# Unscaled attention probabilities, turned by a product with the identity times the inverse sums

## What is computed

```
# block 1, differential attention: 4 heads, two score parts each
s = where(visible, q @ k.T * scale - slope * dist, -inf)
p = softmax(s)
p = p[:, 0] - lam * p[:, 1]
o = p @ v
# block 1, cross attention to 256 memory tokens: 4 heads of 256
p = softmax(q @ k.T * 256 ** -0.5); o = p @ v
# block 2: 8 heads of 64, keys chosen by a top-k index
p = softmax(where(valid, q @ k_sel.T * scale, -inf)); o = p @ v_sel
# block 3, forgetting attention: 8 heads of 64
p = softmax(where(causal, q @ k.T * scale + c_i - c_k, -inf)); o = p @ v
```

## Time and profile before

| | |
|---|---|
| three runs | 2840.22, 2843.74, 2840.40 us, median 2840.40 us |
| the profiled execution | 2841.07 us, span 2839.8 us, mean granted TensorE clock 0.981 |
| PE busy | 2715.2 us, 96% |
| PEld busy | 2328.0 us, 82% |
| DVE / ACT / POOL busy | 1598.5 us (56%) / 1055.0 us (37%) / 639.4 us (23%) |
| diff attention | about 155 to 197 us |
| cross attention | about 501 to 535 us |
| dsa attention | about 1218 to 1271 us |
| fox attention | about 1889 to 1976 us |

### The profile page before, as it was taken

How to read it: one execution, slowest core, us unless ns; L and a number is a source line. 1 busy time by engine, 2 the same in 40 slices (tenths; PEclk the granted TensorE clock), 3 DMA queues, 4 the chain that set the end, 5 groups by cost and what they waited for, 6 DMA issues and landing times. The chain is left out here.

```text
span 2839.8 us, 42561 instructions
## 1 busy us (share of the span) xinstructions
PE 2715.2 (96%) x16614; PEld 2328.0 (82%) x16614; DVE 1598.5 (56%) x2472; ACT 1055.0 (37%) x1823; POOL 639.4 (23%) x507
## 2 busy tenths in 40 slices
PE   8989999999999999989999999999999989999998
PEld 6769876788888777867888888976799889999986
DVE  5875657366653455945533337965544456666643
ACT  4354333442222333262423224546434243422223
POOL 3440101221100223450100003355344210212101
PEclk9999899999999999999999999999999999999998
DMA  4200231122232322202322222210111032222221
GB/s 162 91 8 8 90 104 60 45 90 96 97 100 98 119 74 68 97 23 82 96 98 97 97 97 76 83 45 2 51 35 46 28 119 83 83 96 90 97 97 60
DMA packets 64276, 219.08 MB, mean 77 GB/s; under 512 B 8182, under 2 KB 8822, under 8 KB 63830
## 3 DMA queue, kind: packets, MB, share of 16 engines
q1 hardware_dynamic: 61190, 211.62, 22.7%
q10 hardware_dynamic: 2896, 4.82, 0.5%
HBM read 210.07 MB, written 6.32 MB: 76 GB/s over the span
## 5 line engine op out<-in xcount | busy, mean ns | idle before, releaser
L303 PE MATMUL ps<-normed,slab_parts 128*128 128x512 f32 (+3 forms) x2248 | 773.4, 344 | 26.5 <-DVE normed L645 12.1
L305 PE MATMUL ps<-normed,slab_parts 128*128 128x512 f32 (+3 forms) x2248 | 753.8, 335 | 0.0
L304 PE MATMUL ps<-normed,slab_parts 128*128 128x512 f32 (+3 forms) x2248 | 753.4, 335 | 0.0
L163 ACT ACTIVATE slab_parts<-ring 128x1024 fp32r<-128x1024 f32 x364 | 384.4, 1057 | 890.8 <-PE ps L305 873.9
L167 DVE TENSOR_TENSOR slab_parts<-ring,slab_parts 128x1024 fp32r<-128x1024 f32 x348 | 464.9, 1338 | 377.2 <-ACT slab_parts L163 376.6
L303 PEld LDWEIGHTS ps<-normed,slab_parts 128*128 128x128 f32 x2248 | 427.6, 190 | 80.7 <-issue 23.4
L304 PEld LDWEIGHTS ps<-normed,slab_parts 128*128 128x128 f32 x2248 | 427.7, 190 | 47.5 <-issue 5.3
L305 PEld LDWEIGHTS ps<-normed,slab_parts 128*128 128x128 f32 x2248 | 427.0, 190 | 43.4
L303 PE MATMUL ps<-hidden,slab_parts 128*128 128x512 f32 x560 | 218.5, 390 | 5.6 <-DVE hidden L254 5.6
L305 PE MATMUL ps<-hidden,slab_parts 128*128 128x512 f32 x560 | 218.5, 390 | 0.0
L304 PE MATMUL ps<-hidden,slab_parts 128*128 128x512 f32 x560 | 218.5, 390 | 0.0
(11 more groups left out here) (598 smaller groups left out, 4347.7 us busy)
## 6 DMA issues: line engine op xcount, KB each, us to landing
ring<-in_stream SPq DMA_DIRECT2D x376, 512.0 KB, 3.3
scratch_gates<-fox_y SPq DMA_DIRECT2D x12, 258.0 KB, 2.3
branch_gates<-scratch_gates ACTq DMA_DIRECT2D x1, 2064.0 KB, 14.9
h<-in_x SPq DMA_DIRECT2D x8, 256.0 KB, 6.2
scratch_fox_y<-fox_y SPq DMA_DIRECT2D x1, 1032.0 KB, 7.0
gdn_z<-scratch_gates ACTq DMA_DIRECT2D x1, 1032.0 KB, 6.4
fox_y<-scratch_fox_y ACTq DMA_DIRECT2D x1, 1032.0 KB, 17.1
mix_y<-in_sgu_b SPq DMA_DIRECT2D x1, 1024.0 KB, 6.4
```

Of the source, the lines that this page charges most:

```text
L163: self.nc.scalar.activation(self.hi[:, n % PARTS, :], self.ring[:, n % SLOTS, :], ACT.Copy).then_inc(self.hi_ready, 1)
L303: nc.tensor.matmul(to, lhsT[0], rhs[0], start=start, stop=False)
L304: nc.tensor.matmul(to, lhsT[0], rhs[1], start=False, stop=False)
L305: return nc.tensor.matmul(to, lhsT[1], rhs[0], start=False, stop=stop)
```

## The change

`probs` is no longer scaled. POOL's instruction per unit now multiplies the identity, one tile wide (128x128 or 88x88), by the inverse sums of the unit's rows, into a new buffer `softmax_factors` with four slots. PE turns a tile with a plain matmul: the weights are the unscaled tile of `probs`, and the streamed operand is this scaled identity, so that the product is the turned and scaled tile. With two parts, the factor of the second part becomes minus lambda times the first sum over the second sum (the multiply on line 2207 becomes one with a third operand), DVE's join no longer waits for POOL but for its own inverses, and PE waits for both the join (`joined`) and the factors (`spread`).

```diff
@@ -2128,8 +2128,9 @@
         s = K.buf(local, "scores", [P, 2, parts, kmax * rows]) if bias else None
         pT = K.buf(local, "probsT", [P, 2, kmax, rows])
         stat = K.buf(local, "softmax_stats", [P, KEEP, parts, 4])
-        padded, p_scaled, scored, maxed, exped, inverted, p_ready, turned, pT_out, o_filled, o_out, chain = (K.sem(n) for n in (
-            "att_padded", "p_scaled", "scored", "maxed", "exped", "inverted", "p_ready", "p_turned", "pT_out", "o_filled", "o_out", "att_chain"))
+        factors = K.buf(local, "softmax_factors", [P, KEEP, rows])
+        padded, joined, scored, maxed, exped, inverted, spread, turned, pT_out, o_filled, o_out, chain = (K.sem(n) for n in (
+            "att_padded", "p_joined", "scored", "maxed", "exped", "inverted", "factors_spread", "p_turned", "pT_out", "o_filled", "o_out", "att_chain"))
 
         def bank(u, part, n):
             lo = (u % 2) * 1024 + part * 512
@@ -2154,11 +2155,13 @@
                     last.then_inc(scored, 1)
 
                 def transposes(u):
-                    pe.wait_ge(p_ready, u + 1)
+                    pe.wait_ge(spread, u + 1)
+                    if parts == 2:
+                        pe.wait_ge(joined, u + 1)
                     if u >= sets:
                         pe.wait_ge(pT_out, u - sets + 1)
                     for t in range(units[u][2]):
-                        last = nc.tensor.transpose(turned_at(u, t), p[0:rows, u % KEEP, 0, t * rows:(t + 1) * rows], K.ident[0:rows, 0:rows])
+                        last = nc.tensor.matmul(turned_at(u, t), p[0:rows, u % KEEP, 0, t * rows:(t + 1) * rows], factors[0:rows, u % KEEP, :], start=True, stop=True)
                     last.then_inc(turned, 1)
 
                 def values(u):
@@ -2204,15 +2207,16 @@
                         ins = nc.vector.reciprocal(stat[0:rows, u % KEEP, part, 3:4], stat[0:rows, u % KEEP, part, 2:3])
                         if part == 1:
                             link(ins)
-                            ins = nc.vector.tensor_tensor(stat[0:rows, u % KEEP, 1, 3:4], stat[0:rows, u % KEEP, 1, 3:4], minus_lambda[0:rows, :], ALU.mult)
+                            ins = nc.vector.scalar_tensor_tensor(out=stat[0:rows, u % KEEP, 1, 3:4], in0=stat[0:rows, u % KEEP, 1, 3:4], scalar=minus_lambda[0:rows, :],
+                                                                 in1=stat[0:rows, u % KEEP, 0, 2:3], op0=ALU.mult, op1=ALU.mult)
                         ins.then_inc(inverted, 1)
 
                 def joins(u):
                     keys = units[u][2] * rows
-                    dve.wait_ge(p_scaled, u + 1)
+                    dve.wait_ge(inverted, parts * (u + 1))
                     pp = p[0:rows, u % KEEP]
                     nc.vector.scalar_tensor_tensor(out=pp[:, 0, 0:keys], in0=pp[:, 1, 0:keys], scalar=stat[0:rows, u % KEEP, 1, 3:4],
-                                                   in1=pp[:, 0, 0:keys], op0=ALU.mult, op1=ALU.add).then_inc(p_ready, 1)
+                                                   in1=pp[:, 0, 0:keys], op0=ALU.mult, op1=ALU.add).then_inc(joined, 1)
 
                 if first:
                     first(dve, link)
@@ -2263,14 +2267,8 @@
 
                     nc.gpsimd.memset(pT[HD:value_rows], 0.0).then_inc(padded, 1)
                 for u in range(U):
-                    keys = units[u][2] * rows
-                    pool.wait_ge(inverted, parts * (u + 1))
-                    pp = p[0:rows, u % KEEP]
-                    inv = stat[0:rows, u % KEEP]
-                    if parts == 1:
-                        nc.gpsimd.tensor_scalar(pp[:, 0, 0:keys], pp[:, 0, 0:keys], inv[:, 0, 3:4], None, ALU.mult).then_inc(p_ready, 1)
-                    else:
-                        nc.gpsimd.tensor_scalar(pp[:, 0, 0:keys], pp[:, 0, 0:keys], inv[:, 0, 3:4], None, ALU.mult).then_inc(p_scaled, 1)
+                    pool.wait_ge(inverted, parts * u + 1)
+                    nc.gpsimd.tensor_scalar(factors[0:rows, u % KEEP, :], K.ident[0:rows, 0:rows], stat[0:rows, u % KEEP, 0, 3:4], None, ALU.mult).then_inc(spread, 1)
 
 
 def mixer_1(K, y, ins):
```

## The result

| | before | change |
|---|---|---|
| median of 5 runs each | 2843.74 us | 2861.85 us |
| lowest and highest | 2840.22, 2853.52 | 2854.94, 2868.25 |
| profiled execution, span | 2841.07, 2839.8 | 2860.39, 2859.1 |

A forecast was written before the change was run, and what follows sets the result against it. PE was taken to bound the attentions; one more record per tile gave fox 10.3 + dsa 6.5 + cross 3.3 + diff 1.9 = 22.0 us, so 2862.4 us against 2840.4 us, range 2850 to 2870 us.

The forecast's parts named there:

- What bounds the kernel, and the sign: All four attentions: PE is full in their long stretches, POOL has slack, so the change is slower; over 0.2% slower, chance 0.96.
- One more record per tile: PE's turning: the product is two records where the transpose is one, adding 0.111 us per tile of 128 columns.
- rival B: PE's turning in every stage: the product takes three more record times per tile, not one; 2929 us, chance 0.02.
- Cross: Cross attention: 30 of 32 tiles pay 0.111 us each, two fall into the fill; +3.3 us, ends 3.2 and 3.6.
- Dsa: Dsa attention, 80 tiles: +0.2 us at the first units, 6.3 us for 64 tiles, one-tile units free; +6.5 us.
- Fox: Fox attention, 168 tiles: 9.5 us in the full stretch, 0.8 us from units of three tiles, small units nothing; +10.3 us.
- I take 0.0775 us: Fox: price on PE of one further record of 88 columns, with 0.075 and 0.0875 us as ends.
- the 24 tiles of the small units: Fox's end: their records add 1.9 us against 3.3 us of room on PE, so they cost nothing.
- rival D: Stage ends: the room is a loop through the transposes, so tiles called free pay too; 5 us more, 2867 us, chance 0.06.
- Diff: Diff attention, 40 tiles: +2.0 us at half clock, +1.8 us from 172 to 184 us, -1.9 us of vanished waits; +1.9 us.
- The half-clock stretches should stand where they stood: Whole program: PE's stretches at half clock were expected in the same places after the change as before.
- rival A: Diff's 166 to 172 us and after fox: the fuller PE keeps 2.4 GHz; 2854 us, or 2851 us, chance 0.14.

The follow-up runs named there:

- product_only: The kernel before with a plain matmul with the identity in the transpose's place, POOL still scaling the rows; ratio to before 1.0076.
- turn_only: The change with the transpose put back, factors made but unused, so probabilities are never divided by their sums; ratio to before 0.9966.
- after_again: The changed kernel, unchanged, run again for a second profile; 2860.30 us in one run.
- before_again: The kernel before, unchanged, run again for a second profile; 2849.43 us in one run.
- turn_only_again: turn_only, unchanged, run again for a second profile; 2837.35 us in one run.
- transpose_twice: The kernel before with each transpose issued twice into the same place, a second record without the product; ratio to before 1.0059.

## Why the prediction was right, and where its terms were not

*What bounds the kernel, and the sign: right.* PE is full in the middle of every attention and the change adds a record per tile there. Product_only and turn_only part the two halves: change minus turn_only is 2.9 + 3.3 + 7.8 + 13.9 = 27.8 us in the four stages (part of diff's 2.9 being clock), and turn_only minus before is -5.8 us (again with clock in it).

*One more record per tile: right.* 640 records, 0.111 us for 128 columns, and the doubled transpose costs about the same. The fourfold price of the float32 product (rival B) is refuted: 0.22 us against 0.11 us is twofold. The Trainium skill's "Perfetto Trace Analysis", section Transposes, advises the transpose. The runs agree: with the product alone the kernel is slower by a ratio of 1.0076, 21.6 us.

*Cross: right*, 3.27 us for 3.3, in every execution.

*Dsa: +7.06 us for +6.5.* The clock was alike at its start in both (0.55 and 0.53 in 1218 to 1224 us), so the 0.6 us is the sum's own error, and the starts of the turnings show its parts. To the turning of the third unit it is +0.31 us, where +0.2 was forecast; the 48 tiles of the next fourteen units cost 5.48 us, 0.114 us each and not 0.111; the units of two tiles cost 1.03 us, and 16 x 0.111 less the 0.8 us of room gives 0.98: right; the one-tile units cost 0.25 us and not nothing.

*Fox: +13.94 us for +10.3; the step that failed.* Two terms were mis-sized. "I take 0.0775 us" came from the further record of the values product and of the transpose; the product with 88x88 weights takes more. Units 1 to 23, 114 tiles, went from 47.89 to 57.79 us: +9.90, 0.087 us a tile, the upper end that I had given, and +1.1 us over the term. And "the 24 tiles of the small units ... against 3.3 us of room: nothing" is wrong: they cost 1.75 us (1.5 us in after_again). The units of three tiles grew by 1.64 us, where the sum had 1.5 (eight units, two terms). The rest, 0.65 us, lies before unit 1's turning, where the granted clock was lower:

```profile
1897.00:1905.00 8.00, 5.59 (x20) 2.76 (x21) 3.75 (x13) 3.54 (x7) 1.93 (x3) 0.86 0.00 1
```

Before it was 1.00 in the 8 us from 1889 us on. So rival D was right for fox: the room at its end is, for the most part, no room. A loop that passes through the turning would explain it. The view of one tile's waiters, for the change from 1978 to 1997 us, shows both sides of such a loop:

```profile
its engine sat idle before it (us, times) until:
  POOL softmax_factors L2271: 1.2, 3
  ACT probsT L2248: 0.4, 2
who waited for it (us, times):
  ACT probsT L2248: 1.3, 3
  ACT probs L2238: 1.3, 3
```

PE waits for POOL's factors before the turning, and ACT waits for the turning before its copy and before an exponential (1.3 and 1.3 us, against 0.8 and 0.7 us in the kernel before from 1958 to 1975 us). That exponential gives DVE's sum, from which POOL makes a later factor. The loop is argued from these waits; no run breaks it. The factors aren't needed for it: product_only, in which POOL scales the rows as before, has the same 10.19 us for the units of two tiles. What failed is that I set the sum of PE's idle microseconds in a stretch against the added records. In dsa's units of two tiles I had worked out the room turn by turn, and there it held; its one-tile units, taken by the sum of idle time again, cost 0.25 us. Of the 5 us given for D, fox shows 1.5 to 1.75 us and dsa 0.25 us.

*Diff: -2.25 us for +1.9.* The waits went as forecast: the DVE waits for POOL are gone, and so is PE's half clock for a part. By pieces: to the turning of unit 3 -1.27 us, where +2.0 was forecast; units 3 to 8 +1.60 (forecast +1.8, right); the rest -2.58 (forecast -1.9). The first piece failed, since I took the half clock of 166 to 172 us as a fixed part of the kernel. In the change only the first unit and the scores behind it run at half clock (8 records in 1.97 us), and the next unit's 8 records take 1.09 us:

```profile
162.07 2.05 PE L2164 MATMUL ps<-softmax_factors,probs 128*128 128x128 f32 x8 [1.59 <-DVE probs L2218]
164.04 1.60 PE L2303 MATMUL ps<-diff_qk 64*128 64x384 f32 x4
165.57 1.16 PE L2164 MATMUL ps<-softmax_factors,probs 128*128 128x128 f32 x8
166.66 0.92 PE L2303 MATMUL ps<-diff_qk 64*128 64x384 f32 x4
```

The table of clocks above shows that this moves between executions of one program: before has 0.72 or 0.86, turn_only 0.72 or 1.00. With 0.86 in both, before_again against the change is 41.00 against 39.78 and 39.66 us: -1.3 us. Of these up to 1.1 us is clock again, since the last 2.2 us of before_again's stage were at half clock and the change's were not. So the change's own part in diff lies between -0.2 and -1.3 us, and 1 to 2 us of the -2.25 are clock. The gain of the vanished waits without the product is clearer: before and turn_only_again both ran at half clock from 165.4 to 172 us, and 42.03 against 39.15 us is 2.9 us, of which at most 0.6 us is before's lower clock at the end (its last 1.2 us).

*"The half-clock stretches should stand where they stood": wrong*, and with it the test that a stage without attention may not move by 2 us. The stretch after fox to the end went from 863.77 to 861.25 us; over all executions here it is 860.7 to 866.4 us, and between diff and cross 303.0 to 313.5 us, in kernels with and without the product. Behind fox this is not rival A; for diff and the start of dsa, whether a fuller PE keeps the clock up isn't settled by so few profiles. Right behind fox the change stood at half clock as before did:

```profile
2000.00:2005.00 5.00, 5.00 (x26) 4.87 (x24) 0.70 (x3) 1.73 (x4) 4.05 (x2) 0.50 0.00 0
```

The Trainium skill's "TensorE: Matmul & The Clock Gate", Part 4, says that a transpose doesn't count as busy in the same way for the clock gate. By that the kernels with transposes should have the lower clock. In 162 to 174 us, turn_only (transposes) had 1.00 in one execution and 0.72 in another, and the change 0.86 in two; these runs neither bear the rule out nor refute it.

*The smaller terms.* POOL's instructions last 0.606 and 0.499 us, as forecast. The multiply with a third operand takes 0.220 us and not 0.159, within what was allowed. The median's +18 us lies below the profile's +19.3 us and the sum's 22.0; the rest of the program differs by several microseconds from run to run (the first kernel's own runs spread over 13 us), and the interval to 23 us holds all three.

## What to carry to other kernels

When work moves from an engine that waits to one that is full, count its records on the full one at their exact shape; the doubled instruction and the half of a change run alone give that price in one run each. Idle time of an engine at a stage's thin end is not room as a sum: work it out turn by turn, against what paces the turn, and look at who waits for the instruction before you call it free. Compare stages piece by piece, from one marked instruction to the next, with the granted clock beside each piece: where the clock was equal, the same program repeated to 0.02 us. Run the kernel before a second time before explaining one or two microseconds.

## What the runs showed of the hardware

- A float32 product of 128 columns is two records of 0.111 us, a transpose one of 0.110 us, and a product of fp32r operands one of about 0.12 us.
- With 88x88 weights and 88 columns a record of the product takes 0.084 us, one of the doubled transpose 0.079 us, by the distance of starts in one turn of 12 records.
- Further records at a stage's thin end: in dsa 16 cost 1.03 us of 1.78 and 8 cost 0.25 us of 0.89; in fox 16 cost 0.89 us of 1.34 and 8 cost 0.64 to 0.86 us of 0.67.
- Where the granted clock falls, and for how long, differs between executions of one program. It made up to 2.2 us in diff (turn_only) and 2.5 us in dsa (the change), and nothing in cross; but transpose_twice, run once with a profile, began cross at half clock and lost 1.5 us by it.
- On one column a three-operand instruction of DVE takes 0.220 us, the two-operand multiply 0.159 us:

```profile
L2210 DVE SCALAR_TENSOR_TENSOR softmax_stats<-softmax_stats,minus_lambda 128x1 f32<-128x1 f32 x16 | 3.5, 220 | 0.6
```
